# A four-stage network kernel on one core: element-wise work of the heads moved from VectorE to GpSimd, one level of a small inverse split, and two pieces of the expert and hyena stages shared out anew

## The reference, cut to what matters

```python
# heads, per direction z: decay factors e, keys k, rates a, receptances r, gate g, bonus weight rk
k_z = k * (1 + (a_z - 1) * ka) * faded(e_z)       # keys' fading: one product per direction
bon = sum_head((k_0 + k_1) * r * rk)              # key sum and bonus, late half of the tokens
o   = (norm(y) * lnw + lnb + bon * v) * g         # output rows
T   = (1 - A)^-1, A strictly triangular           # inverse of 64x64 blocks, from 16x16 ones up
# experts
x = x + gate * moe(x)                             # residual's add
# hyena
h = (x * rsqrt(mean(x^2) + eps)) * scale + shift  # first squares, then the scaling per channel
```

## Time and profile before

| what | us |
|---|---|
| median of 3 runs | 1819.65 |
| the profiled execution | 1820.97 |
| its span | 1819.2 |
| PE / DVE / ACT / POOL busy | 1397.8 / 758.5 / 447.9 / 81.8 |
| heads, from their first chain step to the last y | 144.1 to 625.5 |
| layer 0 weights streaming | from 627.8 |

### The profile page before, as it was taken

One profiled execution on the slowest core, in us unless ns is written; L12 is line 12 of the kernel. 1 busy time (PEld: TensorE's weight loads), 2 busy tenths in 40 slices (PEclk: granted clock), 3 DMA queues, 4 the chain that ended last, 5 costly groups with the idle time before them and its releaser, 6 DMA issues. The chain is left out here.

```text
span 1819.2 us, 35613 instructions
## 1 busy us (share of the span) xinstructions
PE 1397.8 (77%) x14647; PEld 763.2 (42%) x14647; DVE 758.5 (42%) x1928; ACT 447.9 (25%) x857; POOL 81.8 (4%) x109
## 2 busy tenths in 40 slices
PE   5878898989886989985466638998899985556545
PEld 2446655665565444432122213776554341222111
DVE  5767777777765366400000001766747510000001
ACT  3244565456544021100000002213121110000001
POOL 0001111111011000000000001000000000000001
PEclk8979999999988999997888779999999997887788
DMA  9023334424345499999999998224289999999995
GB/s 330 3 63 100 101 117 128 122 91 133 118 130 182 138 428 428 426 427 427 428 427 427 428 394 310 93 93 171 75 337 385 423 428 427 427 428 428 427 427 220
DMA packets 108948, 504.56 MB, mean 277 GB/s; under 512 B 16225, under 2 KB 61041, under 8 KB 83953
## 3 DMA queue, kind: packets, MB, share of 16 engines
q1 hardware_dynamic: 107520, 501.93, 69.6%
q10 hardware_dynamic: 1264, 0.33, 0.1%
HBM read 501.13 MB, written 1.09 MB: 276 GB/s over the span
## 5 line engine op out<-in xcount | busy, mean ns | idle before, releaser
L1972 PE MATMUL banks<-arena 128*32 128x512 f32 (+1 forms) x2048 | 324.9, 687 | 242.1 <-DMA arena<-in_moe_w_gate 121.0
L1972 PEld LDWEIGHTS banks<-arena 128*32 128x32 f32 (+1 forms) x2048 | 97.5, 131 | 466.9 <-issue 463.3
L2186 DVE TENSOR_TENSOR arena<-banks,arena 128x512 f32<-128x512 f32 x20 | 13.8, 691 | 631.7 <-PE banks L1972 631.4
L1982 PE MATMUL banks<-arena 128*32 128x512 f32 (+1 forms) x1024 | 146.8, 615 | 33.1 <-DMA arena<-in_moe_w_down 31.0
L795 PE MATMUL banks<-arena 128*128 128x512 f32 (+1 forms) x384 | 159.2, 552 | 0.0
L2100 ACT ACTIVATE arena<-banks,arena 128x128 f32<-128x128 f32 x80 | 30.1, 456 | 303.3 <-PE banks L1959 303.3
L1982 PEld LDWEIGHTS banks<-arena 128*32 128x32 f32 (+1 forms) x1024 | 45.7, 120 | 131.0 <-issue 123.5
L795 PEld LDWEIGHTS banks<-arena 128*128 128x128 f32 x384 | 70.2, 196 | 53.7 <-issue 46.5
L2616 PE MATMUL banks<-arena 128*128 128x256 f32 x384 | 87.4, 386 | 0.0
L2616 PEld LDWEIGHTS banks<-arena 128*128 128x128 f32 x384 | 73.5, 193 | 16.7 <-issue 6.6
L1959 PEld LDWEIGHTS banks<-arena 128*128 128x128 f32 x640 | 73.0, 192 | 16.7 <-issue 14.9
(11 more groups left out here) (415 smaller groups left out, 2337.1 us busy)
## 6 DMA issues: line engine op xcount, KB each, us to landing
arena<-in_moe_w_gate SPq DMA_DIRECT2D x64, 2048.0 KB, 25.4
arena<-in_moe_w_up SPq DMA_DIRECT2D x64, 2048.0 KB, 27.0
arena<-in_moe_w_down SPq DMA_DIRECT2D x56, 2048.0 KB, 25.3
arena<-in_ada_w SPq DMA_DIRECT2D x128, 192.0 KB, 3.0
arena<-in_ada_w SPq DMA_DIRECT2D x64, 256.0 KB, 3.4
arena<-in_moe_w_down SPq DMA_DIRECT2D x32, 512.0 KB, 16.5
arena<-in_rw_wrkv SPq DMA_DIRECT2D x24, 512.0 KB, 5.2
arena<-in_hy_w_in SPq DMA_DIRECT2D x6, 2048.0 KB, 8.4
```

Source lines behind the costliest of these rows:

```text
L1972: mm = pe.matmul(bank[j * rows:(j + 1) * rows, :], xT[:, t, j * rows:(j + 1) * rows], w[:, t], start=(t == 0), stop=(t == KT - 1), tile_po ...
L1982: mm = pe.matmul(bank[j * rows:(j + 1) * rows, :], hT[:, t, j * rows:(j + 1) * rows], w[:, k, half * 512:(half + 1) * 512], start=(t == 0) ...
L2186: dve.tensor_tensor(h, U[:, :], h, ALU.mult).then_inc(h_ready, 1)
```

## The change

In the heads, `key_sum`, the keys' fading, `bonus` and `output` leave VectorE's order for GpSimd's. Two new semaphores, `keys_ready` (VectorE after `key_products`) and `faded_ready` (GpSimd after the second fading), tie them in; `products_early` and the next `decay_rank` wait for `faded_ready` too. `base_level(8)` is cut: its first product and sum stay in slot 13, the second pair goes to slot 15, behind the update of step 4 and the G of step 5; `decay_sum(q, 0)` goes ahead of `turn_out`. ScalarE's `spread` goes from slot 14 to slot 15, behind `rate_rank` and the table load.

```diff
@@ GpSimd
+            def key_sum(n):
+                pool.wait_ge(keys_ready, n + 1)
...
+                pool.tensor_tensor(to, last_steps(KK[n % 2], 0), last_steps(KK[n % 2], 1), ALU.add)
+                pool.drain()
+            def faded_keys(n, z):
+                pool.wait_ge(ex_ready, 2 * n + z + 1)
+                eb = cum[z] if z == 0 else sg[z]
+                pool.tensor_tensor(steps(KK[n % 2], z), steps(KK[n % 2], z), chunks(eb), ALU.mult)
+                if z:
+                    pool.drain()
+                    pool.sem_inc(faded_ready, 1)
+            def bonus(n):
...
+                pool.tensor_tensor(bon[n % 3], bon[n % 3], rT, ALU.mult)
+                pool.drain()
+                pool.tensor_scalar(bon[n % 3], bon[n % 3], vec(8, n), None, ALU.mult).then_inc(bon_ready, 1)
+            def output(n):
+                pool.wait_ge(open_act, OPEN.taken(n, "rows")[1])
+                pool.tensor_tensor(outT[:, 0:L], outT[:, 0:L], vL[n % 3], ALU.mult)
+                pool.tensor_scalar(outT[:, L:TOK], outT[:, L:TOK], vec(6, n), vec(7, n), ALU.mult, ALU.add)
+                pool.drain()
+                pool.tensor_tensor(outT[:, 0:L], outT[:, 0:L], outT[:, L:TOK], ALU.add)
+                pool.drain()
+                pool.tensor_tensor(r.oT[:, n], outT[:, 0:L], gT[n % 3], ALU.mult)
+                pool.drain()
+                pool.sem_inc(o_done, 1)
...
+                if 0 <= n < CH:
+                    key_sum(n)
+                    faded_keys(n, 0)
                 for j in range(STEPS):
                     if 0 <= m < CH and j < STEPS - 1:
                         faded_state(m, j)
+                    if 0 <= n < CH and j == 0:
+                        faded_keys(n, 1)
+                    if 0 <= n < CH and j == 1:
+                        bonus(n)
+                    if m >= 1 and j == 5:
+                        output(m - 1)
@@ TensorE, products_early
+                pe.wait_ge(faded_ready, n + 1)
@@ ScalarE
-                    if now and slot == 14:
-                        spread(n)
                     if early and slot == 15:
                         rate_rank(q, 0)
                         rate_rank(q, 1)
                         act.activation(spare, s.c("ones")[:, 0:1], ACT.Sqrt)
+                    if now and slot == 15:
+                        spread(n)
@@ VectorE
                     if now and slot == 13:
-                        base_level(8, wide)
-                        dve.sem_inc(base_ready, 1)
+                        base_level(8, wide, (0,))
                     if chain and slot == 14:
                         modulate(m, 3)
                     if now and slot == 15:
-                        turn_out(n)
+                        base_level(8, wide, (1,))
+                        dve.sem_inc(base_ready, 1)
                     if early and slot == 15:
                         decay_sum(q, 0)
+                    if now and slot == 15:
+                        turn_out(n)
                     if early and slot == 16:
                         decay_centre(q, 0)
-                    if behind and slot == 16:
-                        output(m - 1)
```

At an expert layer's end, `scatter` takes the banks in the order 0, 2, 1, 3 and waits for the first half of the rows alone (`y_first`) before the first two; VectorE multiplies in the same order and itself adds the second halves, GpSimd only the first ones:

```diff
-            for k in range(4):
+            for nth, k in enumerate((0, 2, 1, 3)):
...
                 dve.tensor_tensor(acc[:, k // 2, c], OUT[k][:, :], gate_b[:, c], ALU.mult).then_inc(out_read, 1)
                 dve.drain()
-                dve.sem_inc(gated, 1)
+                if k % 2 == 0:
+                    dve.sem_inc(gated, 1)
+                else:
+                    dve.tensor_tensor(s.x_res[:, k // 2, c], s.x_res[:, k // 2, c], acc[:, k // 2, c], ALU.add)
+                    dve.drain()
```

In hyena's inputs ScalarE squares the first tile and VectorE the second; ScalarE loads the root's table ahead; `hT` is made by ScalarE (even tiles) and VectorE (odd tiles):

```diff
@@ ScalarE
-            for i in range(TT):
-                act.activation(tmp[:, 0], s.x_res[:, i], ACT.Square, accum_out=stat[:, i:i + 1])
-                act.drain()
+            act.activation(tmp[:, 0], s.x_res[:, 0], ACT.Square, accum_out=stat[:, 0:1])
+            act.drain()
             act.sem_inc(sq_done, 1)
+            act.activation(tmp[:, 0, 0:1], s.c("ones")[:, 0:1], ACT.Sqrt)
...
-            for t in range(KT):
+            for t in range(0, KT, 2):
@@ VectorE
+            dve.tensor_tensor(tmp[:, 1], s.x_res[:, 1], s.x_res[:, 1], ALU.mult)
+            dve.drain()
+            dve.tensor_reduce(stat[:, 1:2], tmp[:, 1], AX.X, ALU.add)
...
+            for t in range(1, KT, 2):
+                dve.wait_ge(xnT_done, t + 1)
+                dve.tensor_scalar(hT[:, t], s.psum[t][:, 0:L], sc[:, t:t + 1], sh[:, t:t + 1], ALU.mult, ALU.add).then_inc(hT_odd, 1)
```

More of the change, by code:

```diff
@@ L646, in rwkv_heads @@
     hf_ready = s.sem("hf_ready")
+    keys_ready, faded_ready = s.sem("keys_ready"), s.sem("faded_ready")
     open_taken, inv_taken = {"act": open_act, "dve": open_dve}, {"act": inv_act, "dve": inv_dve}
@@ L1134, in decay_rank @@
                     act.wait_ge(feat_ready, n)
+                    act.wait_ge(faded_ready, n)
                 act.activation(sg[z], read_inverse(n, f"w{z}")[:, :], ACT.Sigmoid, bias=vec(z, n)).then_inc(inv_act, 1)
@@ L1364, in key_products @@
                 dve.drain()
-            def key_sum(n):
-                if n >= 3:
-                    dve.wait_ge(open_done, OPEN.done(n - 3, "rows"))
-                to = bon[n % 3].rearrange("p (j t) -> p j t", t=C)
-                dve.tensor_tensor(to, last_steps(KK[n % 2], 0), last_steps(KK[n % 2], 1), ALU.add)
-            def bonus(n):
-                dve.tensor_tensor(bon[n % 3], bon[n % 3], rT, ALU.mult)
-                dve.drain()
-                dve.tensor_scalar(bon[n % 3], bon[n % 3], vec(8, n), None, ALU.mult).then_inc(bon_ready, 1)
+                dve.sem_inc(keys_ready, 1)
             def features_a(n, z):
@@ L1386, in features_b, with receptances @@
                 dve.tensor_tensor(steps(BB[n % 2], z), steps(BB[n % 2], z), chunks(eb), ALU.mult)
-            def features_kr(n, z):
-                eb = cum[z] if z == 0 else sg[z]
+            def receptances(n, z):
                 if z == 0:
                     dve.wait_ge(open_act, OPEN.taken(n, "rg")[1])
-                dve.tensor_tensor(steps(KK[n % 2], z), steps(KK[n % 2], z), chunks(eb), ALU.mult)
                 to = late(n % 2, z, 1)
@@ L1579, in row_scales @@
                 dve.tensor_tensor(c4, c4, st[:, 4:8].unsqueeze(2).to_broadcast([P, 4, HEAD]), ALU.mult).then_inc(yn_ready, 1)
-            def output(n):
-                dve.wait_ge(open_act, OPEN.taken(n, "rows")[1])
-                dve.tensor_tensor(outT[:, 0:L], outT[:, 0:L], vL[n % 3], ALU.mult)
-                dve.drain()
-                dve.scalar_tensor_tensor(outT[:, 0:L], outT[:, L:TOK], vec(6, n), outT[:, 0:L], ALU.mult, ALU.add)
-                dve.drain()
-                dve.scalar_tensor_tensor(r.oT[:, n], outT[:, 0:L], vec(7, n), gT[n % 3], ALU.add, ALU.mult)
-                dve.drain()
-                dve.sem_inc(o_done, 1)
             dve.memset(H, 0.0)
@@ L1617, in _ @@
                         features_b(n, 0)
-                        key_sum(n)
-                        dve.drain()
-                        features_kr(n, 0)
+                        receptances(n, 0)
                     if behind and slot == 2:
@@ L1647, in _ @@
                         modulate(m, 2)
-                    if now and slot == 11:
-                        bonus(n)
                     if now and slot == 12:
@@ L2017, in scatter @@
         def scatter(pe, i, par, start=False, stop=False):
-            pe.wait_ge(y_ready, i + 1)
-            for k in range(4):
+            pe.wait_ge(y_first, i + 1)
+            for k in (0, 2, 1, 3):
+                if k == 1:
+                    pe.wait_ge(y_ready, i + 1)
                 pe.matmul(OUT[k][:, :], selwT[par][:, k // 2], y[:, k % 2 * 512:(k % 2 + 1) * 512],
@@ L2371, in _ @@
                     hidden_rows(dve, i)
-                    for k in range(4):
+                    for nth, k in enumerate((0, 2, 1, 3)):
                         c = slice(k % 2 * 512, (k % 2 + 1) * 512)
-                        dve.wait_ge(scat_done, i * 4 + (k + 1))
+                        dve.wait_ge(scat_done, i * 4 + (nth + 1))
                         dve.tensor_tensor(rows_b[:, c], OUT[k][:, :], gate_b[:, c], ALU.mult)
@@ L2382, in _ @@
         def _(pool):
-            for k in range(4):
-                c = slice(k % 2 * 512, (k % 2 + 1) * 512)
-                pool.wait_ge(gated, k + 1)
-                pool.tensor_tensor(s.x_res[:, k // 2, c], s.x_res[:, k // 2, c], acc[:, k // 2, c], ALU.add)
+            for t in range(TT):
+                pool.wait_ge(gated, t + 1)
+                pool.tensor_tensor(s.x_res[:, t, 0:512], s.x_res[:, t, 0:512], acc[:, t, 0:512], ALU.add)
             pool.drain()
@@ L2768, in combine @@
                 op.then_inc(spec_ready, 1)
+            dve.tensor_tensor(tmp[:, 1], s.x_res[:, 1], s.x_res[:, 1], ALU.mult)
+            dve.drain()
+            dve.tensor_reduce(stat[:, 1:2], tmp[:, 1], AX.X, ALU.add)
```

(10 more changed lines are left out.)

45 lines of the change are left out of this document (25 added, 20 removed).

## The result

| | before | after |
|---|---|---|
| median of the executions | 1819.91 us (1818.46 to 1820.27, 4) | 1844.20 us (1843.93 to 1844.64, 3) |
| the profiled execution | 1820.97 | 1844.64 |
| its span | 1819.2 | 1842.8 |
| granted TensorE clock over the span | 0.904 | 0.894 |

What follows compares the result with a forecast made beforehand. A head round was taken as a chain changing hands with no engine full, the expert layers as bound by the weight stream. Heads +6.2, layers' ends +2.0, hyena -1.65 gave +6.5, from 1819.65 to 1826.2 us; range 1813 to 1832.

Steps and rivals of the forecast that it cites:

- `base_ready` 2 us later, the serial line behind it: Heads, steps 5 to 7: `base_ready` at 305.85, not 303.85; spread, transposes, placing, keys follow serially; norm product starts +0.4.
- the hole on ScalarE: Sign in the changed trace: ScalarE idle for over 1 us between the spread and the placing.
- The 0.36 which TensorE now waits for the next state absorbs all but +0.05: Heads, step 6: TensorE's existing 0.36 wait for the state hides most of the norm product's +0.4, leaving about +0.05.
- the +0.55 per round: Heads, rounds 1 to 5: +0.05 for the later norm product plus 0.5 for contention, each round; 2.75 in all.
- rival C: Heads: GpSimd or contention sets the pace, 7 x +1.6 and more, about +15, 1834 us; chance 0.10.
- Rival A: Heads: norm product not held, so the gain is kept, 6 x -1.3 and more, -8.4, 1811 us; chance 0.16.
- `output` against the cut-off half, 0.5: Heads: GpSimd's `output`, about 2.7 us, overlaps VectorE's cut-off half by 1 us and costs 0.5; bounds 0 and 1.1.
- The fading: Heads, steps 1 to 4: the second fading on GpSimd takes near 0.7 us, ends near 274, and `faded_ready` gates nothing.
- Round -1, +2.2: Before round 0: placing starts at 131.2, not 128.59, with part of a gain against it; +2.2, bounds 0 and +3.
- Round 6, +1.2: Heads, round 6: update of step 5 +1.0, placing 2.6 later, partly hidden by load waits; +1.2, bounds -1.5 and +2.7.
- Layers' ends, +1.0 each: End of both expert layers: VectorE gets two more additions of 0.77 and its drain stands last; +1.0 each, +2.0 together.
- Hyena, -1.65: Hyena's inputs: ScalarE makes four `hT`, not eight, so TensorE starts sooner; -1.65, bounds 0 and -3.5.

Runs made afterwards that it cites:

- e2_pool: The kernel before with only the heads' work moved to GpSimd, last level whole in slot 13, spread in slot 14: 1820.64 us, ratio 1.0002.
- e5_warm2: The changed kernel with four idle matmuls of 256 columns, in free columns of bank 7, ahead of the norm product's wait: 1833.87 us, ratio 1.0076.
- e9_after_place: The changed kernel with the second placing's four ScalarE instructions moved, two behind the keys, two behind U of step 6: 1822.66 us, ratio 1.0009.
- e1_order: The kernel before with the level cut in two, decay sum ahead of `turn_out`, spread in slot 15, nothing moved to GpSimd: 1836.54 us, ratio 1.0090.
- e10_best2: The changed kernel with old order of level and spread, GpSimd adding all pieces at the layers' ends, second placing behind the keys: 1812.73 us, ratio 0.9953.
- e6_late_spread: The kernel before with the heads' work moved to GpSimd and the spread in slot 15, the last level whole in slot 13: 1835.11 us, ratio 1.0092.
- e11_before_place: The kernel before with the second placing moved behind the keys, nothing else: 1820.89 us, ratio 0.9999.

## Why the forecast was right in direction and wrong in size

- **`base_ready` 2 us later, the serial line behind it.** Right. The forecast had the norm product 0.4 later in the round, and 0.5 more from the contention; counted from the round's first update it came at 45.36 on the mean of rounds 1 to 5, against 44.34 before, +1.02. Counted so, the last half ended at 34.87 against 32.37, 2.5 later, the 2.0 and the contention's 0.5 together; the hole on ScalarE was over 1 us; the wait for the keys was over 2.
- **"The 0.36 which TensorE now waits for the next state absorbs all but +0.05" and the +0.55 per round: the step that failed.** It priced the wait of 2.4 us as time and left out what the pause does to the clock. Behind the norm product TensorE is the hand of the round, and there half clock costs: 15.44 against 13.84 us. With the pause filled, the best rounds were at 62.1 to 62.2 and the time 10.3 lower. The missing term is about 1.9 a round: 1.6 in the rest of the round and 0.3 in step 6 (8.73 against the 8.40 at full clock). With the forecast's 0.55 that is the 2.4 measured, and over five rounds it is more than half of the miss. What the forecast named as rival C, GpSimd or contention setting the pace, came near by its number (1834) and not by its mechanism: the work on GpSimd alone cost nothing (e2_pool). In round 6, 17.1 us at half clock (573.3 to 590.4) cover step 5 (10.90 against 5.23); that stretch began in a wait of 4.12 us for the modulation's weights, so not all of it is the keys' doing.
- **Rival A.** The gain was not kept, as forecast: steps 4 and 5 together took 18.68 against 19.04.
- **`output` against the cut-off half, 0.5.** Too much. The half's product took 1.08 in round 3 and 1.36 in round 4, against 1.10 before; it was GpSimd's last product that stretched, to 1.63 and 1.40 from 0.73, so that `output` took 3.9 us in round 3 and not 2.7. VectorE gave up 2.3 us a round, where the forecast had about 4. The fading took 1.28 and not 0.7, since it has 512 columns, and still gated nothing, ending at 344.99, 1.7 behind the update.
- **Round -1, +2.2.** Open. The change had +4.57, with a half-clock stretch behind the norm product, 136.4 to 143.3, that before has not; but from 90 us to the first update before had 20.5 us of half clock in all too, the change 22.5. The two runs without the full pause had +3.1 (e5_warm2) and +3.3 (e9_after_place), the order alone (e1_order), with a pause of 2.75, only +1.1.
- **Round 6, +1.2.** Open. The same two runs had -0.9 and -2.1, but the two kernels with the old heads lie at -0.5 and +3.7 there, so no term of this size can be judged.
- **Layers' ends, +1.0 each.** Mechanism right (VectorE's drain is the last of the engines', at 1149.7 and 1832.5), size wrong: +1.67 each, because the two sums were priced at 0.77 and the first took 1.42 beside GpSimd; and +1.3 at layer 0 from the loop's slower turns, which no row of before could tell.
- **Hyena, -1.65.** -1.85 by the trace, and layer 1 kept it (-0.08).

The Trainium skill (GPSIMD Engine Reference, Engine selection) holds that two-input work belongs on VectorE; e2_pool (ratio 1.0002) agrees in so far as moving it paid nothing by itself; the fastest kernel here, e10_best2, has it all the same.

## What to carry to other kernels

Price a wait of TensorE twice: the time itself, and the half-clock stretch behind it, above all where TensorE-bound work follows. Several short waits with work between them can cost less than their sum in one place: with waits of 1.7 to 2.0 and 0.4 to 0.8 (e1_order) two of rounds 1 to 5 had the half clock behind the norm product, with one wait of 2.44 all five. So taking work off another engine can make things slower by merging waits. Before moving anything, list what stands in a serial line without being needed by it: one helper moved out of the keys' way here was worth 21.5 us in the changed kernel and nothing in the kernel before.

## What was not expected of the hardware

- The granted clock fell to 0.50 behind a pause of 2.44 us at the same place in six rounds out of six. Behind 1.0 to 1.1 it did so in three of six (e6_late_spread), behind 0.44 to 0.58 in two of six (before). With the pause filled to 0.2 to 0.55 it did so in one of six (e5_warm2), and with no pause in none of eighteen (e9_after_place, e10_best2, e11_before_place).
- An empty loop of six turns on VectorE's sequencer took 0.54 or 0.70 us a turn at the same place of the program, 0.70 in the kernels with the heads' work on GpSimd; why is open.
- In the experiments one kernel's executions lay up to 16.3 us apart (1814.7 to 1831.1 for e11_before_place), those of before up to 14.4 on one chip, those of e10_best2 5.6 us and of e9_after_place 4.2 us.
